# Exchanging the halves of a rotary turn by four queue transfers instead of a permutation matmul

## What is computed

```
def rope(x, pos):
    d = x.shape[-1]
    inv_freq = ROPE_THETA ** (-jnp.arange(0, d, 2, dtype=jnp.float32) / d)
    ang = pos.astype(jnp.float32)[:, None] * inv_freq[None, :]
    cos, sin = jnp.cos(ang).astype(x.dtype), jnp.sin(ang).astype(x.dtype)
    x1, x2 = x[..., : d // 2], x[..., d // 2:]
    return jnp.concatenate([x1 * cos - x2 * sin, x2 * cos + x1 * sin], axis=-1)
...
    def block(qblk):
        s = jnp.einsum('cbhqd,cbhkd->cbhqk', qblk, k).astype(jnp.float32)
        p = jax.nn.softmax(s, axis=-1)
        w = p[0] - lam * p[1]
        return jnp.einsum('bhqk,bhkv->bhqv', w.astype(v.dtype), v)
```

## Time and profile before

| | us |
|---|---|
| Median of three executions | 4220.1 (4216.68 to 4224.41) |
| The profiled execution, its own time | 4215.4 |
| Its span from the first to the last instruction | 4213.5 |
| Mean granted clock of TensorE | 0.956 of full |
| Second block, about | 2330 to 4213 |
| TensorE busy over the span | 3787.8 |
| VectorE, ScalarE, GpSimd busy | 1880.3, 1452.4, 990.4 |

### The profile page before, as it was taken

The page is one execution under the profiler, slowest core; times in us unless marked ns, Lnnn a source line. Parts: engine busy times, 40 slices in busy tenths (PEclk is TensorE's granted clock), DMA queues, the critical chain, the costliest instruction groups (busy, mean ns, idle before and its releaser), DMA issues.

```text
span 4213.5 us, 76305 instructions
## 1 busy us (share of the span) xinstructions
PE 3787.8 (90%) x34140; PEld 2315.6 (55%) x34140; DVE 1880.3 (45%) x2057; ACT 1452.4 (34%) x1831; POOL 990.4 (24%) x438
## 2 busy tenths in 40 slices
PE   6989999999999999999899888988978888988977
PEld 3556666666665665547455445555544455545544
DVE  3456454655555654250423336335352255345352
ACT  4222223232322312231212244444533344444542
POOL 2413223233424332131143210111102300111102
PEclk9999999999999999999999998999989999989999
DMA  2111111111111112333231200010102200100102
GB/s 98 51 37 46 42 46 47 48 51 47 52 42 52 46 57 101 134 121 110 95 130 40 88 26 12 21 41 16 36 6 92 71 17 12 36 26 16 41 29 83
DMA packets 61624, 227.56 MB, mean 54 GB/s; under 512 B 6832, under 2 KB 8560, under 8 KB 60784
## 3 DMA queue, kind: packets, MB, share of 16 engines
q1 hardware_dynamic: 52224, 189.64, 13.3%
q10 hardware_dynamic: 9072, 33.03, 2.0%
HBM read 174.93 MB, written 47.71 MB: 53 GB/s over the span
## 4 chain that ended last, share of the span: by engine, by line
PE 72%; DVE 14%; ACT 8%; POOL 2%; issue 2%; DMA 1%; ACTq 0%; DVEq 0%; SPq 0%; POOLq 0%
PE psum L1037 70%; DVE arena L2169 5%; ACT arena L1624 5%; DVE arena L2172 4%; PE psum L1040 2%; DVE arena L2640 2%; POOL arena L2699 1%; ACT wh L1624 1%; DMA arena<-in_w_proj_conv 1%; ACT arena L2103 1%; POOL hl L2699 1%; DVE arena L2574 0%; DVE arena L2176 0%; DVE arena L2549 0%; POOL wl L2699 0%
## 5 line engine op out<-in xcount | busy, mean ns | idle before, releaser
L1037 PE MATMUL psum<-arena 64*64 64x32 f32 (+13 forms) x23468 | 1390.8, 255 | 264.9 <-ACT arena L1624 91.8
L1037 PEld LDWEIGHTS psum<-arena 64*64 64x64 f32 (+8 forms) x23468 | 993.2, 140 | 683.6 <-issue 370.8
L2699 POOL TENSOR_TENSOR wl<-arena,wh 128x1024 bf16<-128x1024 f32 x203 | 493.6, 2432 | 2190.5 <-ACT wh L1624 2186.9
L1037 PE MATMUL psum<-hh,wh 128*128 128x512 f32 x3248 | 917.0, 426 | 72.3 <-ACT hh L1624 24.6
L1037 PE MATMUL psum<-hh,wl 128*128 128x512 bf16 x3248 | 820.4, 393 | 1.6 <-POOL wl L2699 1.6
L1624 ACT ACTIVATE arena<-psum 128x512 f32<-128x512 f32 (+4 forms) x660 | 415.8, 630 | 1132.9 <-PE psum L1037 819.5
L1037 PE MATMUL psum<-hl,wh 128*128 128x512 bf16 x3248 | 766.4, 382 | 8.0 <-POOL hl L2699 8.0
L1037 PEld LDWEIGHTS psum<-hh,wh 128*128 128x128 f32 x3248 | 615.8, 196 | 277.8 <-issue 52.6
L2169 DVE TENSOR_TENSOR arena<-psum,arena 128x512 f32<-128x512 f32 (+3 forms) x472 | 299.8, 635 | 961.6 <-PE psum L1037 531.9
L2172 DVE SCALAR_TENSOR_TENSOR arena<-arena 128x1024 f32<-128x1024 f32 x356 | 574.9, 1615 | 196.6 <-ACT arena L1624 182.1
L2699 POOL TENSOR_TENSOR arena<-arena 128x1024 f32<-128x1024 f32 (+4 forms) x142 | 362.4, 2552 | 856.3 <-ACT arena L1624 488.3
(11 more groups left out here) (38 smaller groups left out, 774.9 us busy)
## 6 DMA issues: line engine op xcount, KB each, us to landing
arena<-in_w_in SPq DMA_DIRECT2D x161, 512.0 KB, 3.6
scr_g<-arena ACTq DMA_DIRECT2D x24, 512.0 KB, 2.6
arena<-scr_g SPq DMA_DIRECT2D x24, 512.0 KB, 4.4
arena<-in_w_out SPq DMA_DIRECT2D x24, 512.0 KB, 3.5
arena<-in_w_mem_kv SPq DMA_DIRECT2D x16, 512.0 KB, 3.5
scr_x<-arena SPq DMA_DIRECT2D x16, 512.0 KB, 3.6
arena<-scr_x SPq DMA_DIRECT2D x16, 512.0 KB, 7.3
arena<-in_x SPq DMA_DIRECT2D x8, 512.0 KB, 10.6
```

What stands on the lines that cost most here:

```text
L1037: return pe.e.matmul(o, l, r, start=start, stop=stop)
L2699: return pool.seq.tensor_tensor(o, a, b, op)
```

## The change

The permutation on TensorE goes, and with it the pair of banks that it held and the use of `PX` as the product's place. Instead SyncE waits for `dq_copy` (and for the previous turn's add, which frees the tile) and issues four transfers from `PX` to a new tile `SWAP`, 32 partitions by 1024 fp32 each (128 KB), with the halves exchanged. VectorE waits for the fourth landing, multiplies `SWAP` by the sines in place (both operands now in SBUF), and only then waits for the cosines and adds. `SWAP` lies where the fourth head's output is put later. The table `TURNS` is the same.

```diff
@@ tiles
+    SWAP = sl(5120, 1024)
@@ qk_ready
-            held(("rope", L, h, i), ("rope", L, h, i))
+            do("rope", L, h, i)
             yield 0.25
             do("turned", L, h, i)
-            ps.leave(("rope", L, h, i))
@@ tensor_program
-        def rope(L, h, i):
-            use = ("rope", L, h, i)
-            pe.wait_ge(*at("dq_copy", L, h, i))
-            sums(use, "rope", perm, PX)
@@ vector_program
         def turned(L, h, i):
-            use = ("rope", L, h, i)
-            dve.wait_ge(*at("rope", *use))
+            dve.wait_ge(*at("swapped", L, h, i))
             dve.wait_ge(*at("consts2"))
+            tt(SWAP, SWAP, sin, MUL).then_inc(*dve.up("rope_sin", L, h, i))
+            x = QK[h % 2][i]
             dve.wait_ge(*at("rope_cos", L, h, i))
-            tt(PX, pair(use), sin, MUL).then_inc(*dve.up("rope_sin", L, h, i))
-            ps.give(use, ("rope_sin", L, h, i))
-            x = QK[h % 2][i]
-            tt(x, x, PX, ADD).then_inc(*dve.up("rope_add", L, h, i))
+            tt(x, x, SWAP, ADD).then_inc(*dve.up("rope_add", L, h, i))
@@ sync_program
+        def rope(L, h, i):
+            sp.wait_ge(*at("dq_copy", L, h, i))
+            if h or i:
+                sp.wait_ge(*at("rope_add", L, h - 1 + i, 1 - i))
+            for j in range(4):
+                a, b = slice(32 * j, 32 * j + 32), slice(32 * (j ^ 1), 32 * (j ^ 1) + 32)
+                sp.e.dma_start(SWAP[a], PX[b]).then_inc(*(sp.land("swapped", L, h, i) if j == 3 else sp.land("swapped", L, h, i, j)))
```

More of the change, by code:

```diff
@@ L1537, in tensor_program @@
                     matt=matt, sv_turn=sv_turn, ga_up=ga_up, diag=diag, lev=lev, kt=kt, st=st, so=so, so_sum=so_sum,
-                    dv_turn=dv_turn, rope=rope, qk=qk_, dt=dt, dv=dv, do_sum=do_sum)
+                    dv_turn=dv_turn, qk=qk_, dt=dt, dv=dv, do_sum=do_sum)
         for name, *a in plan:
@@ L2935, in sync_program @@
         does = dict(init=init, load=load, lora_load=lora_load, fetch=fetch, mem_load=mem_load, q_load=q_load, x_load=x_load,
-                    back_o=back_o, back_u=back_u, x_store=x_store, consts2=consts2, small_load=small_load, sg_out=sg_out, mix_load=mix_load,
+                    back_o=back_o, back_u=back_u, x_store=x_store, consts2=consts2, rope=rope, small_load=small_load, sg_out=sg_out, mix_load=mix_load,
                     xr_load=xr_load, resid=resid, store=store)
```

## The result

Eight runs of each kernel: median 4239.6 us after the change (4228.4 to 4250.9), 4220.8 before (4214.5 to 4227.2). The ratio is 1.0045, with a 95% interval of 1.003 to 1.006: 19 us slower. The profiled execution took 4240.9 us, its span is 4239.0 (before 4215.4 and 4213.5), the mean granted clock 0.947 (before 0.956).

The account below looks back on a forecast made before the run. TensorE was taken to bound the kernel, with short detours through other engines. Layer 0 (+2.5) and layer 1 (+5.5) sum to +8.0 us, 4223.4 for the profiled execution; forecast 4228 against the median 4220.1, range 4217 to 4243.

Parts of the forecast that it names:

- the queue's delay on the chain: Between dq_copy and VectorE's start: SyncE's queue replaces the permutation, making a turn 1.05 us later.
- T: Time from the end of dq_copy to the fourth transfer's landing: 3.5 us, each 0.1 us worth 1.2 us of kernel.
- the rival with slow transfers: The four transfers do not overlap or move at half rate: T 4.2 to 5.1, 4236 to 4247 us; chance 0.13.
- The first head's turns: Head 0, both turns: earlier transposes against late sk load and low clock; -0.8 us in layer 0, +0.75 in layer 1.
- Turn (1,0): Head 1, first turn: later start, but the add no longer slowed by GpSimd; 0.1 us later in each layer.
- Turns (1,1) and (3,1): Second turns of heads 1 and 3: 1.05 us later each, nothing won, TensorE's wait growing to 6.6 us.
- Turns of head 2: Head 2: first turn wins 1.4 us of TensorE's work, second loses 1.05; together 0.35 won per layer.
- (3,0): Head 3, first turn: later start against an add no longer slowed by GpSimd; 0.1 us later in each layer.
- The clock: Longer TensorE waits bring the low clock level at the scores: 1.4 us more at three sites and at (0,1) in each layer.
- What the permutation cost: Sixteen permutations are 22 us of TensorE's work, of which 2.8 us were said to be on the path.

Follow-up runs that it names:

- Interleaved, four: Changed kernel with rotation partners laid beside each other and four transfers of every fourth partition, 128 KB each: 4229.6 us, 1.0027 of the kernel before.
- Eight transfers: Changed kernel with eight transfers of 16 partitions, 64 KB each, for a turn instead of four of 32: 4275.4 us, 1.0135 of the kernel before.
- Two queues: Changed kernel with transfers 2 and 3 issued by ScalarE instead of SyncE, right behind dq_copy: 4247.8 us, 1.0079 of the kernel before.
- Second turns only: Changed kernel with transfers only at each head's second turn; first turns keep the permutation: 4231.7 us, 1.0036 of the kernel before.
- No exchange: Changed kernel with neither transfers nor permutation; the sine product reads PX itself, halves not exchanged: 4214.5 us, 0.9985 of the kernel before.
- Sines in place: Kernel before, sine product written over the permutation's banks without waiting for GpSimd's cosines, add reading those banks: 4206.6 us, 0.9980 of the kernel before.
- Transfers and matmuls: Changed kernel plus the permutation's matmuls, result unread, banks free when the matmuls end: 4254.1 us, 1.0089 of the kernel before.
- Both: Changed kernel plus the permutation's matmuls, result unread, banks held until the sine product ends: 4255.0 us, 1.0091 of the kernel before.
- the best kernel by transfers: Changed kernel with neighbouring partners, two transfers of every second partition, and weight loads ahead at first turns of heads 0, 1, 3: 4210.7 us, 0.9986.
- both interleaved kernels: Changed kernel with neighbouring partners: four transfers of every fourth partition (4229.6 us, 1.0027) or two of every second, 256 KB each (4217.9 us, 0.9997).
- Loads first: Changed kernel with the weight load behind the first turns of heads 0, 1 and 3 issued ahead of the transfers: 4232.5 us, 1.0035 of the kernel before.
- Sines early: Kernel before, permutation kept, sine product written into SWAP without waiting for GpSimd's cosines: 4209.5 us, 0.9984 of the kernel before.

## Why the prediction came out as it did

The direction was right, and so was the main cause: the queue's delay on the chain and the low clock at the scores. The time came 11.6 us above the forecast, inside the range. That it came so near is in part luck: summed by turns the loss was four times the forecast, and what brought it down was a gain that the prediction had put at nothing. In its terms:

**T was mis-sized.** Forecast 3.5, measured 4.18 at most turns. Half of the error is the issues: I took 0.48 each from eight loads in a row, they are 0.61 to 0.64. The other half is the landing: 2.34 against the small load's 2.0. This is the start of the rival with slow transfers (T 4.2 to 5.1, 4236 to 4247), and there the time lies, the ratio 1.0045 on 4220.1 being 4239.

**What T is worth.** Four kernels differ mainly in T (and in the order of channels, and in how long the issues hold up the load behind them): 2.98 us behind the copy gives 0.9997, 3.90 gives 1.0027, 4.20 gives 1.0045, 6.72 gives 1.0135. From end to end that is 0.0138 over 3.74 us, 58 us over 3.74: 1.6 us for each 0.1 us of T, where the prediction had 1.2. On the line between 2.98 and 3.90, a product at 3.55 (T = 3.5) gives 1.0016, or 7 us, where 8 were forecast. So the size of T is the term that was off as far as the total goes. The terms by turns below were off as well, and that they and the stalls nearly cancel at T = 3.5 is luck.

**The bound on T.** From the second on, the issues begin 0.63 to 0.64 us apart whether a packet takes 165, 284 or 390 ns ("Interleaved, four", the changed kernel, "Eight transfers"): the issue is a bound of its own, which neither half the bytes nor faster data lowers. "Interleaved, four" changes neither bytes nor count, and begins 0.3 us sooner at 165 ns a packet instead of 284: 32 neighbouring partitions are slow to move. By "Two queues" this data time takes over where the issues are closer. Both come out near 0.6 us for a transfer. From the ports that the Trainium skill (SBUF, "Door 1: The DMA port swizzle") gives to partitions 0 to 31, 8 of 16, the prediction had an estimate of 0.6 us for such a transfer and of T = 4.1. The measured T of 4.18 lies near it, but the issues alone, 1.84 us for the fourth and 2.34 for its landing, give the same T, so T doesn't confirm it; the slower packets agree with it in direction.

**The first head's turns** were to win 0.8 us in layer 0 and lose 0.75 in layer 1; against the trace of before they lost some 4 and 6.5. The transposes did come 3.5 and 3.3 us earlier (forecast 3.3). But `sq` started 9.6 and 8.7 us behind `dq_copy`, not 7.6: the load of `sk` was issued 2.6 and 2.5 us behind the copy (forecast 1.95) and landed 4.8 and 3.9 us later (3.6). The clock was low behind this new wait too: the first twelve matmuls of `sq` took 5.5 and 4.6 us instead of 3.1. I had looked at the clock at the scores alone.

**Turn (1,0)** was to cost 0.1 us and cost 3.7 in layer 0, 1.7 in layer 1. The add was not slowed, as forecast (1.23 us, all sixteen). But in layer 0 GpSimd's subtraction for the late weights (`wl`) now lay beside VectorE's next operation, the merge of the two softmax halves (`dw`), which took 3.18 us instead of 1.28 before:

```profile
2563.85 2.56 DVE L2164 TENSOR_TENSOR arena<-arena 128x1024 f32<-128x1024 f32 x2 [7.27 <-DMA arena<-arena]
...
2566.24 2.36 POOL L2692 TENSOR_TENSOR wl<-arena,wh 128x1024 bf16<-128x1024 f32 x1 [5.21 <-ACT wh L1619]
2566.51 3.18 DVE L2167 SCALAR_TENSOR_TENSOR arena<-arena 128x1024 f32<-128x1024 f32 x1
```

The collision that I counted as gone had moved by one operation. In both layers this turn's transfers also landed a microsecond late (last section).

**Turns (1,1) and (3,1)**: forecast 1.05 late each, measured 1.77, by T. The waits are 7.88 us (forecast 6.6; the permutation's span is 1.98, not 1.4, and T). **Turns of head 2**: the first won 1.3 in layer 0 (forecast 1.4) and 0.1 in layer 1, where its transfers were late (last section) and `dw` again met GpSimd's subtraction (3.49 us); the second lost 1.75 (1.05). **(3,0)** lost 0.7 to 0.8 (0.1).

**The clock** at the scores went low where I said, at 1.8 us a place instead of 1.4. Summed by turns, the loss is some 31 us against a forecast of 8.0; from the second block's start to the end the time grew by some 29. Between the two lie the waits without a releaser, 8.5 us less than before, and some 7 us of the other sign spread over places outside the turns, of which I followed only a part. The largest gain, 7 us between 3755 and 3790, is two such waits of 2.06 and 2.59 us that only the kernel before has, and the clock for the rest.

**TensorE's waits without a releaser** are the term that the prediction put at nothing. Every one of them over 1 us, 73 in the fourteen kernels here, ends 1.2 to 1.6 us after a packet of 16 KB on the instruction queue has ended, and 70 of the 73 stand right behind a row of small matmuls (64x32 or 32x32). So TensorE had very likely run out of instructions. In the five kernels that have the permutation at second turns these long waits sum to 10.6 to 15.8 us, in the nine that leave it out there to 4.0 to 7.3. The permutation's matmuls make TensorE's program longer and move what comes behind them; why just these waits go with them isn't shown.

The first of them, and the same `lev` step after:

```profile
3759.96 1.36 PE L1037 MATMUL psum<-arena 64*32 64x32 f32 x121 [4.08 <-ACT arena L1624]
3763.39 0.33 PE L1037 MATMUL psum<-arena 64*32 64x32 f32 x7 [2.06 <-issue]
...
3775.61 4.32 PE L1037 MATMUL psum<-arena 64*32 64x32 f32 x44 [2.59 <-issue]
```

```profile
3789.61 1.44 PE L1037 MATMUL psum<-arena 64*32 64x32 f32 x128 [4.08 <-ACT arena L1619]
```

The same 128 matmuls end after 3.76 us in one and 1.44 in the other. Over all kernels they take 1.4 to 1.5 us in the nine without the permutation at second turns, "Second turns only" among them, and 2.1 to 4.0 in the five with it. This isn't the clock: in the kernel before the first 121 run as fast as in the changed one, and the rest stand behind the wait.

**What the permutation cost** is so not nothing, but little. "No exchange" wins 6 us, with 8.8 us less of these waits, against which stand the low clock at the scores and its slower adds. "Sines in place" keeps the permutation, lets the sine product go without GpSimd, and wins 8, within the other's interval.

**What stays open.** "Transfers and matmuls" and "Both" agree at 1.009, 19 us above the changed kernel. Their waits without a releaser of over 1 us sum to 15.5 and 15.8 us against its 4.7, which is 11 of the 19; 4.3 of the 8.7 us between 3750 and 3826 are two of them. The permutation's own time at (0,0) and (2,0) should be a part of the rest; no run parts it further.

## What to carry to other kernels

Work that an engine does inside a wait costs little: before moving it, find what the consumer waits for last. Here that was `dq_copy`, GpSimd and VectorE, and untying VectorE from GpSimd, a change of a few lines, won as much (8 us) as the best kernel by transfers (6 us, the intervals overlap). Look too for waits of TensorE that the profile puts down to "issue": they move with the length of its program, and a change that takes instructions away can win or lose them. Price a chain of small transfers by issue spacing times count plus one landing, and check which partitions each one touches; fewer, wider transfers spread over all partitions took T from 4.2 to 3.0. And where a late load moves a GpSimd operation, look at what it meets next on VectorE.

## What the runs showed of the hardware

**A fetch of instructions delays a transfer.** At three of the sixteen turns, the first ones of (0,1), (1,1) and (1,2), the product began 5.24, 5.14 and 5.74 us behind the copy instead of 4.2. In exactly these three a packet of the instruction queue, 16 KB, ran among the transfers, for 0.92 to 1.03 us; in none of the thirteen others did one. (At (0,0,0), 0.2 us late, one of 8 KB on the other instruction queue did.) The queues of the changed kernel in the 5.3 us of turn (0,1,0):

```profile
q1 hardware_dynamic: 254, 0.78, 61.0%
q8 instruction: 1, 0.02, 1.1%
```

In "Eight transfers" and both interleaved kernels the same three turns had such a packet, and were 0.4 to 2.0 us late, but for one where it began 0.4 us before the landing. Where the packet moved, the delay moved: in "Two queues" turn (1,2,0) had none and was not late, and in "Both" and "Transfers and matmuls" turn (1,3,0) had one and was 1.1 and 1.3 us late.

**A fetch of instructions stops TensorE.** 73 waits of over 1 us without a releaser in fourteen kernels, each ending 1.2 to 1.6 us behind a 16 KB packet of the instruction queue. Most such packets (268 or 269 in each kernel) are followed by none.

**TensorE's clock behind a wait.** The first score matmul takes 0.69 us at 2.4 GHz and 1.22 at 1.2 GHz. By the idle time ahead of it, over all the kernels here: at 2.1 to 2.7 us it took 0.69 to 0.73 at all twelve places (at four of them the clock fell within the next seven matmuls, and the eight took 2.7 to 3.3 us instead of 1.99); at 3.01 us 0.69 at three and 0.81 at one (the kernel before); at 3.9 and 4.8 us, ten places, 0.69 at one, 1.02 and 1.04 at two, 1.22 at seven; at 4.5 us and longer in the kernels that leave the permutation out at second turns, 1.22 at all 52. In a gap of 6.1 us with the permutation's matmuls in its middle it was 0.69 at three of four places (before), without them 1.22 at four of four ("No exchange").

**VectorE's price beside GpSimd** depends on its operands: with both in SBUF beside GpSimd's bfloat16 subtraction, 1.23 us becomes 1.85 to 3.4; with one operand in PSUM it stayed 1.22 to 1.23 in all of "Sines in place", six adds of which run beside that subtraction. The slowed operations are held until GpSimd is through: in the kernel before, the changed one, "Loads first", "No exchange" and "Sines early" all 24 that I compared, the merge `dw` among them, end 1.08 us behind the subtraction's end, however early they began.
